# One layer of a diffusion backbone: keeping attention output, merged chunks and x1 on chip in the two one-block groups

## What is computed

```python
mod = silu(cond) @ w_ada + b_ada                      # sh1, sc1, g1, sh2, sc2, g2
z = (rms_norm(x, norm1_g) * (1 + sc1) + sh1) @ w_in   # q, k, v of two attentions, and gate logits
o_g = gqa_attention(q_g, keys_g, vals_g)
o_d = rms_norm(diff_attention(q_d, keys_d, vals_d, lam), subln_g) * (1 - lam_init)
gate_a, gate_b = split(sigmoid(gate_logits), 2)
merged = gate_a * (o_g @ w_branch_a) + gate_b * (o_d @ w_branch_b)
x = x + g1 * (merged @ w_out)                         # this x is "x1" below
h2 = rms_norm(x, norm2_g) * (1 + sc2) + sh2
x = x + g2 * peer_layer(h2, w_query, sub_keys, expert_u, expert_v)
y = rms_norm(x, final_norm_g)
```

## Time and profile before

| | |
|---|---|
| median of 3 runs | 5383.33 us (5380.68 to 5390.74) |
| profiled execution, its own time | 5383.42 us |
| its span, first to last instruction | 5381.8 us |
| TensorE, matmuls | 3353.9 us (62%) |
| VectorE | 2689.2 us (50%) |
| GpSimd | 1840.4 us (34%) |
| ScalarE | 415.6 us (8%) |
| DMA | 1895.48 MB, 352 GB/s over the span |

### The profile page before, as it was taken

The page is one execution under the profiler, slowest core; times in us unless marked ns, Lnnn a source line. Parts: engine busy times, 40 slices in busy tenths (PEclk is TensorE's granted clock), DMA queues, the critical chain, the costliest instruction groups (busy, mean ns, idle before and its releaser), DMA issues.

```text
span 5381.8 us, 33098 instructions
## 1 busy us (share of the span) xinstructions
PE 3353.9 (62%) x11312; PEld 1269.7 (24%) x11312; DVE 2689.2 (50%) x3921; ACT 415.6 (8%) x785; POOL 1840.4 (34%) x1354
## 2 busy tenths in 40 slices
PE   4586979899688789699988385000333333333566
PEld 0033434344244333344443142000000000000000
DVE  1231013988433301176767775999566565565200
ACT  0011001000022210100010011000000000000000
POOL 0000001444423100044435443666554544544333
PEclk8797989999799989799999697555555555555567
DMA  9984875889999588699999996889999999999998
GB/s 391 393 319 172 295 256 208 324 342 352 360 363 360 233 300 288 245 375 355 375 356 378 366 368 254 363 353 375 421 419 419 419 418 421 419 418 419 417 414 365
DMA packets 415081, 1895.48 MB, mean 352 GB/s; under 512 B 30566, under 2 KB 34182, under 8 KB 243806
## 3 DMA queue, kind: packets, MB, share of 16 engines
q0 software_dynamic: 186848, 1347.98, 61.7%
q1 hardware_dynamic: 228096, 545.82, 27.5%
HBM read 1851.38 MB, written 43.61 MB: 352 GB/s over the span
## 4 chain that ended last, share of the span: by engine, by line
DMA 43%; PE 33%; DVE 15%; issue 5%; POOL 3%; ACT 1%; SPq 0%; DVEq 0%; POOLq 0%; ACTq 0%; PEldq 0%
PE ps L705 26%; DMA activations<-in_peer_v,zt 24%; DVE big L1713 5%; DMA big<-in_peer_v,zone 4%; DMA big<-in_w_ada 4%; DMA big<-in_peer_u,sel 4%; DMA big<-in_peer_v,sel 2%; PE ps L1003 2%; DMA big<-in_peer_v,zt 1%; DVE big L1470 1%; POOL big L688 1%; PE ps L794 1%; DVE big L1417 1%; POOL big L645 1%; PE ps L733 1%
## 5 line engine op out<-in xcount | busy, mean ns | idle before, releaser
L705 PE MATMUL ps<-big,activations 128*128 128x512 f32 x4096 | 1801.0, 600 | 95.1 <-ACT zt L1014 37.1
L1713 DVE CUSTOM_DVE_ANT_0 big<-big,activations 128x2048 f32<-128x2048 f32 x384 | 867.5, 2290 | 503.3 <-DMA big<-in_peer_u,sel 483.5
L705 PEld LDWEIGHTS ps<-big,activations 128*128 128x128 f32 x4096 | 780.0, 192 | 1101.5 <-issue 1020.0
L688 POOL DMA_INDIRECT big<-in_peer_u,sel x384 | 568.5, 1481 | 580.0 <-DVE zt L1713 495.2
L1003 PE MATMUL ps<-activations 128*32 128x512 f32 x1536 | 357.2, 1022 | 455.2 <-DMA activations<-in_peer_v,zt 455.2
L1003 PE MATMUL ps<-big,activations 128*32 128x512 f32 x1536 | 345.7, 994 | 438.4 <-DMA big<-in_peer_v,zt 436.5
L634 POOL DMA_DIRECT2D work<-scores x40 | 23.9, 598 | 1078.6 <-DMA scores<-zone 1014.8
L1407 DVE CUSTOM_DVE_ANT_0 big<-big 128x2048 f32<-128x2048 f32 x128 | 291.4, 2292 | 152.4 <-DMA big<-in_peer_u,sel 110.2
L1417 DVE SCALAR_TENSOR_TENSOR big<-big,work 128x2048 f32<-128x2048 f32 x128 | 301.1, 2352 | 86.6 <-DMA big<-in_peer_v,sel 83.4
L663 POOL DMA_INDIRECT big<-in_peer_u,sel x128 | 227.8, 1780 | 310.2 <-DVE zone L1470 272.8
L645 POOL DMA_INDIRECT big<-in_peer_v,sel x128 | 238.1, 1860 | 275.4 <-DVE big L1417 216.6
(11 more groups left out here) (191 smaller groups left out, 2381.8 us busy)
## 6 DMA issues: line engine op xcount, KB each, us to landing
big<-in_w_in SPq DMA_DIRECT2D x84, 2048.0 KB, 12.4
big<-in_w_ada SPq DMA_DIRECT2D x48, 2048.0 KB, 12.7
big<-in_w_out SPq DMA_DIRECT2D x24, 2048.0 KB, 11.9
big<-in_peer_w_query SPq DMA_DIRECT2D x24, 2048.0 KB, 12.7
big<-in_w_branch_a SPq DMA_DIRECT2D x12, 2048.0 KB, 8.3
big<-in_w_branch_b SPq DMA_DIRECT2D x12, 2048.0 KB, 7.9
big<-z_blocks SPq DMA_DIRECT2D x20, 512.0 KB, 11.7
big<-in_peer_u,sel POOLq DMA_INDIRECT x640
```

What stands on the lines that cost most here:

```text
L688: pool.indirect_dma_start(u_slot(m), None, eu, bass.IndirectOffsetOnAxis(ap=sel[:, t % 2, k:k + 1], axis=0)).then_inc(u_in[m % UR], 16)
L705: ins = nc.tensor.matmul(bank(bk), acts[:, k, b * P:(b + 1) * P], w[:, n % WS, k], start=(start and k == 0), stop=(stop and k == KT // 2 - 1))
L1713: V.tensor_tensor_reduce(out=x, in0=x, in1=h_of[ph], scale=1.0, scalar=0.0, op0=ALU.mult, op1=ALU.add, accum_out=dots_b[ph % 2][:, st * TO ...
```

## The change

- The attention output is transposed by TensorE straight from `onat` in the one-block groups; it is neither stored nor loaded. For this the sample's attention takes its blocks in the order 1, 2, 3, 0, so that block 0 is the last and still in `onat`. Blocks 1 to 3 are stored as before.
- Each merged chunk is written to a place of its own in `zone` (`merged`), and TensorE transposes chunk by chunk (`quarter`).
- x1 stays in the four slots of `zt`, and `norm` reads it there. It is still stored to `x1d`, since the final sums need it.
- The three rows of the norm are loaded during the output projection, after the second chunk's residual, into places that are free then; in group 1 the store of the context's result goes there too.
- The sub-keys' transposes move behind the branches. Their load moves ahead of the queries' load in the context's attention; for the sample it comes after the first two weight halves, together with two loads for `final`.
- Group 2 keeps its ways through DRAM.

```diff
-        narrow = ((ac(A1 + 3 * D, D),), hcur, zn(0, D), zn(D, D), acc)
+        narrow = ((zt_f[:, 0:D],), hcur, ac(A1 + 3 * D, D), ac(A1, D), acc)
...
+        merged = [zn(CH * i, CH) for i in (1, 2, 3, 5)]
...
+        ORDER = ((SB,), (1, 2, 3, 0))
...
                     keys(0)
+                    sp.dma_start(skn.rearrange("p (c d) -> p c d", c=2 * PH), sub).then_inc(sk_in, 16)
...
-                if g < 2:
-                    sp.wait_ge(att[g]["st"], 16 * (1, NB)[g])
-                    if g:
-                        sp.wait_ge(sum_st, 16 * NQ * NQ)
-                        sp.dma_start(acc, vsd).then_inc(fa_in, 16)
-                    sp.dma_start(skn.rearrange("p (c d) -> p c d", c=2 * PH), sub).then_inc(sk_in, 16)
+                if g == 1:
+                    sp.wait_ge(att[1]["o"], NB)
                 half(H_BR[g], 0, 0, br(0, 0))
                 half(H_BR[g] + 1, 0, 0, br(0, 1))
...
                 if g == 1:
+                    sp.wait_ge(sum_st, 16 * NQ * NQ)
+                    sp.dma_start(acc, vsd).then_inc(fa_in, 16)
                     sp.dma_start(ac(A1 + 2 * D, D), x1d[SB]).then_inc(fa_in, 16)
-                    sp.wait_ge(sk_t, 8)
-                    sp.dma_start(ac(A1 + 3 * D, D), mod[1:2, 5 * D:6 * D].to_broadcast([P, D])).then_inc(fa_in, 16)
+                    sp.dma_start(skn.rearrange("p (c d) -> p c d", c=2 * PH), sub).then_inc(sk_in, 16)
...
                 def merged_out(c, i):
-                    for lb in range(n):
+                    for lb in range(n if g == 2 else 0):
...
+                    if g < 2 and c == 1:
+                        sp.wait_ge(mm_done, U_OUT[g])
+                        sp.wait_ge(sk_t, 4 * (g + 1))
+                        if g == 1:
+                            sp.wait_ge(y_ready, 1)
+                            sp.dma_start(yp[0], ac(A1 + 2 * D, D)).then_inc(y_out, 16)
+                        norm2_rows()
...
-                    pe.wait_ge(sk_in, 16 * (g + 1))
-                    for i in range(4):
-                        for j in range(4):
-                            ins = nc.tensor.transpose(bank(4 + i)[:, j * P:(j + 1) * P], skn[:, (4 * i + j) * HD:(4 * i + j + 1) * HD], ident[:, :])
-                        ins.then_inc(sk_t, 1)
-                    pe.wait_ge(sk_e, 4 * (g + 1))
+                    pe.wait_ge(att[g]["o"], (1, NB)[g])
+                    transposes(T_O[g], onat)
...
+                if g < 2:
+                    pe.wait_ge(sk_in, 16 * (g + 1))
...
+                    for q in range(4):
+                        pe.wait_ge(sk_e, 4 * g + q + 1)
+                        pe.wait_ge(G["br"], B * DCH + q + 1)
+                        quarter(T_M[g], q, merged[q])
...
+                if g >= 2:
+                    dve.wait_ge(s["x"][b % 2], 16 * (b // 2 + 1 + R))
...
-                        signal(V.tensor_tensor(zn(lb * CH, CH), zn(lb * CH, CH), gb, ALU.add), G["br"], c * n + (B * DCH + lb + 1))
+                        signal(V.tensor_tensor(zn(lb * CH, CH) if g == 2 else merged[c], zn(lb * CH, CH), gb, ALU.add), G["br"], c * n + (B * DCH + lb + 1))
```

More of the change, by code:

```diff
@@ L244, in build @@
         ada_mm, ada_free, ada_out = sem("ada_mm"), sem("ada_free"), [sem(f"ada_out{i}") for i in range(3)]
-        nrm = [dict(x=[sem(f"n{s}_x{i}") for i in range(2)], row=sem(f"n{s}_row"), h=sem(f"n{s}_h"))
+        nrm = [dict(x=[sem(f"n{s}_x{i}") for i in range((0, 2, 2)[s])], row=sem(f"n{s}_row"), h=sem(f"n{s}_h"))
                for s in range(3)]
@@ L443, in attention @@
                         sp.dma_start(dst, zs[SB, :, lo:lo + n]).then_inc(kv_out, 16)
-                for b in range(blocks):
-                    blk = b if p else SB
-                    if b:
-                        sp.wait_ge(a["qt"], 4 * (p + b))
-                        queries(b)
-                        sums_out(b - 1)
-                        sp.wait_ge(a["o"], p + b)
-                        sp.dma_start(osd[blk - 1], onat).then_inc(a["st"], 16)
+                for b in range(1, blocks):
+                    sp.wait_ge(a["qt"], 4 * (p + b))
+                    queries(b)
+                    sums_out(b - 1)
+                    sp.wait_ge(a["o"], p + b)
+                    sp.dma_start(osd[ORDER[p][b - 1]], onat).then_inc(a["st"], 16)
                 if p:
                     sums_out(SB - 1)
-                sp.wait_ge(a["o"], p + blocks)
-                sp.dma_start(osd[blk], onat).then_inc(a["st"], 16)
             for g in range(3):
@@ L913, in _ @@
                         release(u + (3 + p_) * n)
[L915 removed]
+                if g < 2:
+                    pe.wait_ge(sk_in, 16 * (g + 1))
+                    for i in range(4):
+                        for j in range(4):
+                            ins = nc.tensor.transpose(bank(4 + i)[:, j * P:(j + 1) * P], skn[:, (4 * i + j) * HD:(4 * i + j + 1) * HD], ident[:, :])
+                        ins.then_inc(sk_t, 1)
+                    for q in range(4):
+                        pe.wait_ge(sk_e, 4 * g + q + 1)
+                        pe.wait_ge(G["br"], B * DCH + q + 1)
+                        quarter(T_M[g], q, merged[q])
+                for lb in range(n if g == 2 else 0):
                     first = (n + 1 - lb % 2) // 2
[L917 removed]
+                    pe.wait_ge(G["nat"][lb % 2], 16 * (first + lb // 2 + 1))
                     transposes(T_M[g] + lb, zn((lb % 2) * D, D))
@@ L1144, in _ @@
                     attention(g)
-                    for i in range(4):
-                        sa.wait_ge(sk_t, 4 * g + i + 1)
-                        nc.scalar.activation(misc[:, i * 512:(i + 1) * 512], bank(4 + i), ACT.Copy).then_inc(sk_e, 1)
                 for lb in range(n):
@@ L1169, in _ @@
                     branch(c)
+                for i in range(4 if g < 2 else 0):
+                    sa.wait_ge(sk_t, 4 * g + i + 1)
+                    nc.scalar.activation(misc[:, i * 512:(i + 1) * 512], bank(4 + i), ACT.Copy).then_inc(sk_e, 1)
                 for lb in range(n):
@@ L1606, in _ @@
                 if g < 2:
-                    with ch.loop(DCH, 2 * n) as c:
+                    for c in range(DCH):
                         merge(c)
```

89 lines of the change are left out of this document (47 added, 42 removed).

## The result

The changed kernel takes 5315.57 us (median of 4 runs, 5311.06 to 5317.52) against 5384.11 us (4 runs of the kernel before on the same chip, 5380.68 to 5390.74). The ratio is 0.9872, with a 95% interval of 0.986 to 0.9884: 68.5 us faster. The forecast was 5319.0, the range 5293 to 5333. The profiled execution took 5315.76 us (span 5314.1), 67.7 less than the span of before.

The account below looks back on a forecast made before the run. The prediction took TensorE's products and hand-overs, then a fixed last stage of expert gathers, to bound the kernel. Gains of 23.2 + 16.5 + 20.1 + 3.0 + 1.6 = 64.4 took 5383.4 to 5319.0 us, range 5293 to 5333.

Parts of the forecast that it names:

- A, context: Context's hand-over from attention to branches: first product 23.7 us earlier, less 0.5 for the sub-keys' load; gain 23.2.
- A, sample: Sample's hand-over from attention to branches: raw gain 22.5 us, less a weight stall and clock loss; gain 16.5.
- B, both: Hand-over from branches to output projection, both groups: no DRAM trip, faster first chunk; gains 10.2 and 9.9, together 20.1.
- C, context: Context's hand-over from output to query projection: norm 12.2 us earlier, less 7.5 for displaced transfers and 1.7 clock; gain 3.0.
- C, sample: Sample's hand-over from output to query projection: norm 13.3 us earlier, less 10.0 for four transfers and 1.7 clock; gain 1.6.
- It waits 4.6 us: Sample's branches: TensorE waits 4.6 us for the third weight half, behind two rows and the sub-keys.
- This queue has no slack there: Output projection: early rows delay the weight half behind them, by 7.5 us in the context and 10.0 in the sample.
- its first chunk was slow before and will be: Query projection: its first chunk, 16.57 us before, stays slow, so nothing is gained there.
- Free transfers (1): Rival: displaced transfers cost nothing, so stalls and their clock losses go; 27 us more gain, 5292; chance 15%.
- Larger stalls (2): Rival: late issues add some 4 us at each of three stalls; 5331; chance 13%.
- The clock that stays low (3): Rival: after stalls TensorE's clock stays low for 5 chunks, costing 70 us; kernel slower at 5389; chance 2%.
- That the gain does not arrive (4): Rival: something else, such as block 0's gathers, sets the last stage's start; up to 5380; chance 2%.

Follow-up runs that it names:

- after: The changed kernel itself, against the kernel before: 5315.57 us, ratio 0.9872.
- Experiment 6: Changed kernel with the sample's loads of v_sums, x1 and sub-keys issued one per branch chunk, not all before the third weight half: 5311.14 us.
- Experiment 4: Changed kernel with the merged chunks stored to DRAM and loaded back again, sub-keys' transposes still ahead: 5334.41 us.
- Experiment 8: Changed kernel with one norm row (context) or two (sample) after the second output chunk, remaining rows and context-result store after the third: 5303.57 us, one run.
- experiment 1: Changed kernel with the three norm rows and the context-result store issued after the third output chunk's residual, not the second's: 5298.09 us.
- experiment 5: Changed kernel with x1 loaded back from DRAM for the norm, rows still early: 5320.5 us.
- 9: Changed kernel with the sample's loads spread, one norm row after the second output chunk, two rows and context-result store after the third: 5297.29 us.
- experiment 2: Changed kernel with norm rows and context-result store issued after the last store of x1, x1 still on chip: 5320.51 us.
- 7: Changed kernel with norm rows, then the context-result store, after the third output chunk's residual, and the sample's loads spread: 5290.95 us.
- experiments 3: Changed kernel with the attention output stored to DRAM and loaded back in both groups, sub-keys left in their new places: 5345.59 us.

## Why the prediction was right

The path held at every step. One reading was false (a queue without slack), three sizes were off (two waits for weights too long, the clock's loss too small), and what they did to the sum nearly cancels. Point by point, gains in us of the profiled executions:

| step | forecast | measured | how |
|---|---|---|---|
| A, context | 23.2 | 23.3 | first product at 485.22 for 505.74, plus 2.8 that the kernel was already late there (below) |
| A, sample | 16.5 | 18.1 | attention's end to branches' end 190.5 for 208.6 |
| B, both | 20.1 | 20.9 | 8.6 + 2.1 in the context, 8.3 + 1.9 in the sample |
| C, context | 3.0 | 3.8 | second output chunk's start to query's 67.66 for 71.48 |
| C, sample | 1.6 | 1.6 | the same, 70.84 for 72.45 |
| first branch chunk, context | 0 | 1.7 | 14.01 for the 15.72 of the earlier trace rows |
| first query chunks | 0 | 4.5 | 14.02 for 16.57, and 14.02 for 15.93 |
| the rest | 0 | -6.2 | see below |
| sum | 64.4 | 67.7 | |

**A.** The 4.6 us from attention to first product stand in the chain of after, as forecast. In the sample the first half decided with 8.2 instead of 8.9. The step that failed in size is the stall: "It waits 4.6 us", for the third half. It was 2.4 us less the usual 0.4, so 2.0. For a part the third half was there sooner (27.6 us after the attention for 29.2), for a part TensorE came to it later, since its first chunk was slow. Experiment 6 shows that the loads in front were its cause: with them elsewhere the wait was gone. The clock took some of it back. The forecast has 15.7 us for the first chunk, as before the change, and 1.4 lost behind the wait; it was 17.05, so 1.35 more, and 1.7. That makes 22.5 + 0.7 - 2.0 - 1.35 - 1.7 = 18.1.

**B.** The product came 5.2 after the last branch product in both groups, forecast 5.7. The eight copies are the path, as worked out. (By the forecast's own numbers the sample would have been 9.7, not 9.9: both the shorter chain and the less slow first chunk come off.) Experiment 4 brought 8.5 + 2.4 and 8.1 back, near the 8.6 + 2.1 and 8.3 + 1.9 of the table.

**C.** "This queue has no slack there" was the false step, by one row. It rests on a misread row. In the earlier trace rows the weight load was idle for 1.13 us with the landing of `in_w_out` as its releaser, but one chunk earlier, with no such releaser, it was idle for as long, and TensorE's own pause was 0.33 against the usual 0.30. And right behind the issue of this half at 729.51 the queue was far from full, 170 GB/s where the next window has 399:

```profile
726.70 0.30 PEld L705 LDWEIGHTS ps<-big,activations 128*128 128x128 f32 x2 [1.10 <-issue]
...
730.00:735.00 5.00, 5.00 (x13) 2.13 (x12) 0.00 (x0) 0.00 (x0) 0.00 (x0) 1.00 0.85 170
735.00:740.00 5.00, 5.00 (x13) 2.24 (x12) 0.00 (x0) 0.00 (x0) 0.00 (x0) 1.00 1.06 399
```

Experiment 8 gives the slack: 0.6, 2.65, 5.4 and 8.6 for one to four transfers. So the waits were 5.4 and 8.6, not 7.5 and 10.0. That the sum still came out is due to the second wrong size: the slow chunk behind each wait lost 3.1 (17.05 against 13.97), not 1.7. (The 1.7 was low already: 36.59 - 35.0 is 1.6, and a burst of 80 without a pause ahead takes 34.60 in the trace before, at 939.40, so that burst had lost 2.0.) In the context 7.5 + 1.7 = 9.2 stood for 5.4 + 3.1 = 8.5; in the sample 11.7 for 11.7. Two errors that cancel are not a confirmed price, and only the experiments on the place of the rows tell them apart. The Trainium skill's "DMA: Bandwidth & Descriptors", Specifications, has some 358 GB/s of HBM for a core, by which a row would be 2.9 us. The window of the fourth chunk's wait shows 396 GB/s, above it, and 423 GB/s make a row 2.5; the average of 2.7 per transfer lies between, but it holds SyncE's issues too and does not decide. The Trainium skill's "DMA: Bandwidth & Descriptors", Bandwidth, has 425 GB/s for a transfer of 16 MB, and says that its figures are those of a core whose pair's other core is idle; the windows of this trace are nearer to that one.

**Clock.** "its first chunk was slow before and will be" was wrong, and the 4.5 us that this brought are luck. The query projections' first chunk took 14.0 in after, but 16.3 and 15.9 in experiment 1, where the norm's transposes waited as long in the context (12.27) and a little longer in the sample (14.08). With the context's first branch chunk 6.2 us came from first chunks that the forecast has at nothing. That they match the 6.2 lost in the next paragraph is chance.

**The rest.** The kernel was 2.8 us late already at the last z store ahead of the context's keys (431.08; in the chain of before the store starts at 428.28), which no edit touches. 1.4 goes ahead of the sample's attention (1386.80 for 1424.79 at the keys' first transpose, after 820.79 for 860.18 at the sample's first product), and 0.8 comes back in it. 1.4 is gained in group 2's own transposes. Up to group 2's first product after has gained 72.1 (2213.32 for 2285.46). Then 2.3 are lost in its first 96 instructions (43.80 for 41.46) and 3.6 more until the last stage's first load (3236.72 for 3302.92), and the last stage is 1.5 shorter: 67.7 at the end.

**Rivals.** Free transfers (1) fell: with the rows out of the way 17 us more are to be had, so they were not free. But what spoke for it was real: about one of the transfers is nearly free. Larger stalls (2) fell: one wait each, none at a second chunk behind the fourth. The clock that stays low (3) fell: the chunk after each slow one took 14.0, but for the sample's second gate chunk (15.69), which had a wait of its own ahead. That the gain does not arrive (4) fell: 72.1 at group 2, 67.7 at the end. But "each microsecond taken out of a hand-over should be a microsecond of the kernel" holds only to some us. From group 2's first product to the last stage's first load it took 1014.4 us in experiment 5, 1023.5 in experiment 4 and 1023.4 in after, with the others in between, though no experiment's edit touches it; the last stage took 2077.4 to 2081.4.

## What to carry to other kernels

A trip through DRAM between two stages of TensorE cost 5 to 20 us here. Where it was short (x1 and the merged block), store and load are most of the price, some 7 us in the chain each time. Where it was long (the attention output, 19.8), two weight halves stood in the same queue between them: look first for what stands there. In this kernel a load moved ahead of the streamed weights is paid at TensorE from the second one on, so put it behind the last half that a chunk waits for and as far ahead of its use as it needs, and look at what then stands behind it (here the quarter of x, 1.8 to 2.9 us). The same three rows one chunk later were worth 17 us, a quarter of the whole change. Where an estimate comes out right, undo its terms one by one: keeping x1 on chip (5 us a group, and nothing with late rows) and moving its rows (nearly a draw) look quite different alone than in the sum. And an idle time with a releaser is a wait only for what it has over the usual idle time in the same place.

## What was not expected of the hardware

The first chunk after a pause takes 14.0 us or up to 17.06, and the length of the pause does not tell which. That it is the clock can be seen in after, in the chunk of 17.05 behind the wait for weights (two windows at 0.50, then 0.98) and in the query's first chunk of 14.00 behind the norm:

```profile
713.50:716.50 3.00, 3.00 (x4) 1.45 (x5) 0.00 (x0) 0.00 (x0) 0.00 (x0) 0.50 1.05 387
716.50:719.50 3.00, 3.00 (x4) 1.03 (x4) 0.00 (x0) 0.00 (x0) 0.00 (x0) 0.50 1.05 394
719.50:722.50 3.00, 3.00 (x8) 1.34 (x7) 0.00 (x0) 0.00 (x0) 0.00 (x0) 0.98 1.06 393
...
747.00:761.00 14.00, 13.88 (x32) 6.00 (x32) 0.00 (x0) 0.07 (x1) 0.00 (x0) 1.00 0.41 137
```

Behind the context's transposes with 6.58 idle it took 14.0 in after and experiments 4, 8 and 9, and 15.6 to 16.1 in 1, 2, 5, 6 and 7. Behind the norm with 12.27 idle it took 14.0 in both groups of after and experiments 3 and 4, in the context of 6 and in the sample of 8, and 16.0 to 16.6 in the context of 1, 7, 8 and 9 and in the sample of 6 and 9. Behind 24.8 idle it took 14.0 in experiment 2, and behind 24.6 in the kernel before 16.6. When the pause comes seems to count: where the context's keys started at 437.2 to 437.9 the chunk behind the attention took 14.0 in four of five kernels, and where they started at 434.7 to 435.6 it took 15.6 or more in all four. So what a kernel was ahead there it lost again. That is a correlation of nine profiles, each of one execution, and no run moves the start alone. The Trainium skill's "TensorE: Matmul & The Clock Gate", Part 1, says that the gate watches a window that runs freely and does not start with the kernel, so that the same program can pay for a different number of slow matmuls. The rows agree with that in so far as the same pause of 12.27 us cost 0 to 2.6 us here; that such a window is the reason no run shows.
